# A fused two-block transformer kernel: the recurrent mixer's inputs are loaded ahead of the conditioning chunks, and the chunks' products move later

## The reference, cut to what matters

```python
# block 1
h = rms_norm(x, g_mix); proj = h @ w_in            # 24 column blocks; some for the attention, some for RWKV
r, d_w, k, v, d_a, d_g = split(token_shift_mix(proj_rwkv, mu))     # p + (prev - p) * mu
decay = exp(-exp(-softplus(-(w0 + tanh(d_w) @ w_decay_up)) - 0.5))
a = sigmoid(a0 + d_a @ w_aicl_up);  g = sigmoid(d_g) @ w_gate_lora_up
kk = k * k_k;  kk = kk / max(sqrt(sum(kk * kk)), 1e-12)            # per head of 64: the "key root"
k = k * (1 + (a - 1) * k_a);  b = kk * a
# per head: state = state * decay - (state kk) b^T + v k^T ;  y = state r ; group norm, bonus, times g
x = x + concat(y_dsa, y_rwkv) @ w_out;  x = x + moe(rms_norm(x))
# block 2 uses
mod = silu(c) @ w_ada + b_ada                      # w_ada: 2048 x 12288, six parts of 2048 columns
```

## Time and profile before

| | |
|---|---|
| median of 3 runs | 3314.17 us (3312.25 to 3314.31) |
| the profiled execution | 3311.56 us, its span 3309.3 us |
| mean granted TensorE clock | 0.971 of full |
| PE busy | 94% of the span |
| end of the input projection's matmuls | about 446 us |
| first transposes of `rwkv` (line 962) | 539.7 us |
| pairwise products of `rwkv` (line 977) | 555.0 us |

### The profile page before, as it was taken

The page is one execution under the profiler, slowest core; times in us unless marked ns, Lnnn a source line. Parts: engine busy times, 40 slices in busy tenths (PEclk is TensorE's granted clock), DMA queues, the critical chain, the costliest instruction groups (busy, mean ns, idle before and its releaser), DMA issues. The chain is left out here.

```text
span 3309.3 us, 43832 instructions
## 1 busy us (share of the span) xinstructions
PE 3100.6 (94%) x17864; PEld 2459.1 (74%) x17864; DVE 2067.7 (62%) x2331; ACT 1508.7 (46%) x1819; POOL 20.1 (1%) x10
## 2 busy tenths in 40 slices
PE   8999957979899999999999998999998999999997
PEld 7888844947677676666688876787776788888886
DVE  4557536354677868685548857765575655555555
ACT  4335422223465656564444455455444444444443
POOL 0000001100000000000000000000000000000000
PEclk9999978989899999999999999999999999999999
DMA  7989876076787879696276653475665655555552
GB/s 270 331 274 329 274 263 249 4 296 233 259 315 267 313 256 341 229 320 212 93 248 209 208 194 126 163 241 172 240 230 191 209 185 190 186 182 190 185 183 76
DMA packets 358321, 739.09 MB, mean 223 GB/s; under 512 B 19977, under 2 KB 118422, under 8 KB 344583
## 3 DMA queue, kind: packets, MB, share of 16 engines
q1 hardware_dynamic: 342916, 711.64, 62.5%
q10 hardware_dynamic: 15236, 25.06, 2.1%
HBM read 710.00 MB, written 26.65 MB: 223 GB/s over the span
## 5 line engine op out<-in xcount | busy, mean ns | idle before, releaser
L286 DVE TENSOR_TENSOR moe_w_lo<-ring,moe_w_hi 128x1024 fp32r<-128x1024 f32 x384 | 464.0, 1222 | 174.5 <-ACT moe_w_hi L276 165.4
L286 DVE TENSOR_TENSOR mx_w_lo<-ring,mx_w_hi 128x1024 fp32r<-128x1024 f32 (+1 forms) x288 | 347.5, 1210 | 307.9 <-ACT mx_w_hi L276 303.7
L276 ACT CAST moe_w_hi<-ring 128x1024 fp32r<-128x1024 f32 x384 | 402.3, 1049 | 285.0 <-PE psum L302 281.3
L276 ACT CAST mx_w_hi<-ring 128x1024 fp32r<-128x1024 f32 (+1 forms) x288 | 297.5, 1037 | 448.0 <-PE psum L302 432.0
L286 DVE TENSOR_TENSOR mlp_w_lo<-ring,mlp_w_hi 128x1024 fp32r<-128x1024 f32 x256 | 313.5, 1225 | 293.1 <-ACT mlp_w_hi L276 292.0
L276 ACT CAST mlp_w_hi<-ring 128x1024 fp32r<-128x1024 f32 x256 | 268.4, 1049 | 418.2 <-PE psum L302 418.2
L302 PE MATMUL psum<-mx_w_hi,mx_a_hi 128*128 128x496 f32 (+1 forms) x1024 | 405.6, 396 | 6.4 <-DVE mx_w_lo L286 4.6
L302 PE MATMUL psum<-mx_w_lo,mx_a_hi 128*128 128x496 f32 (+1 forms) x1024 | 397.6, 388 | 0.0
L302 PE MATMUL psum<-mx_w_hi,mx_a_lo 128*128 128x496 f32 (+1 forms) x1024 | 397.6, 388 | 0.0
L286 DVE TENSOR_TENSOR in_w_lo<-ring,in_w_hi 128x628 fp32r<-128x628 f32 x192 | 155.3, 813 | 185.8 <-ACT in_w_hi L276 184.6
L302 PE MATMUL psum<-in_w_hi,in_a_hi 128*128 128x314 f32 x768 | 244.1, 318 | 1.4 <-DVE in_w_lo L286 1.2
(11 more groups left out here) (596 smaller groups left out, 5594.6 us busy)
## 6 DMA issues: line engine op xcount, KB each, us to landing
ring<-in_w_ada SPq DMA_DIRECT2D x72, 1024.0 KB, 7.6
ring<-in_w_e_gate SPq DMA_DIRECT2D x64, 1024.0 KB, 5.4
ring<-in_w_e_up SPq DMA_DIRECT2D x64, 1024.0 KB, 6.3
ring<-in_w_e_down SPq DMA_DIRECT2D x64, 1024.0 KB, 5.2
ring<-in_w_up SPq DMA_DIRECT2D x64, 1024.0 KB, 5.2
ring<-in_w_down SPq DMA_DIRECT2D x64, 1024.0 KB, 5.1
ring<-in_w_in SPq DMA_DIRECT2D x64, 992.0 KB, 5.1
ring<-in_w_in SPq DMA_DIRECT2D x96, 628.0 KB, 5.5
```

The costliest lines, as they stand in the source:

```text
L276: self.nc.scalar.copy(self.w[0][:, self._half(j, half), :, 0:cols], self.view[:, slot, ks, 0:cols]).then_inc(self.hi_done, 1)
L286: self.nc.vector.tensor_tensor(self.w[1][:, q, :, 0:cols], self.view[:, j % self.slots, ks, 0:cols], self.w[0][:, q, :, 0:cols].bitcast(F3 ...
```

## The change

SP no longer asks for chunks 48 to 55 at the end of `first_stream`. It asks for them in `rwkv`, after all inputs of that stage. On ACT the root moves ahead of the two gate copies, and `ada.leave` goes behind the twelve transposed copies. On PE the four chunks at the start and the two behind each gate product are gone. The eight behind the decay sums stay (they are now chunks 48 to 55). Four follow transpose group 14 and four follow group 15. The wait for the copy out of bank 7 moves from ahead of the pairwise products to ahead of group f = 3 of them.

```diff
 # first_stream, SP, at its end
                 sp.wait_ge(da.ov_left, len(da.pairs))
-                ring.first(sp, next_weights)
                 sp.wait_ge(zeroed, 16)
                 in_dram(sp, blocks)
 # program
-        ada.begin()
         rwkv(chip, actT, ada, src["wout"])
 # rwkv, SP, behind the last input
                 sp.dma_start(masks[:], d["consts"][:, RW0:HG0]).then_inc(masks_in, 16)
+                chip.ring.first(sp, ada.source)
+                ada.begin()
                 ada.load(sp, 72)
 # rwkv, ACT
+                root(nc, stat[:], norm[:], asked, rooted)
                 for t in range(T):
                     sc.wait_ge(made, 5 + t)
                     nc.scalar.copy(gate[:, t]..., bank[:, 4:6]...).then_inc(gate_left, 1)
-                root(nc, stat[:], norm[:], asked, rooted)
...
-                ada.leave(sc)
                 for f in range(12):
                     ...
+                ada.leave(sc)
 # rwkv, PE
-                ada.use(pe, 4)
                 pe.wait_ge(small, 2)
...
                         mm = nc.tensor.matmul(bank[:, 4 + b], low[0:LG - P, 3, tt], gup2[:, n], ...)
                     mm.then_inc(made, 1)
-                    ada.use(pe, 2)
...
                     if f == 15:
+                        ada.use(pe, 4)
                         pe.wait_ge(xT_dve, 1)
...
                     mm.then_inc(xT_turned, 1)
+                ada.use(pe, 4)
                 pe.wait_ge(xT_act, 12)
                 pe.wait_ge(xT_dve, 4)
-                pe.wait_ge(ada.copied, 4)
                 for f in range(8):
                     t, qh, kind = f // 4, f // 2 % 2, f % 2
+                    if f == 3:
+                        pe.wait_ge(ada.copied, 4)
```

More of the change, by code:

```diff
@@ L534, in __init__ @@
         self.bank = lambda part: chip.psum[:, 7]
-    def source_next(self, i, j):
-        return self.source(i, self.SPARE + j)
     def source(self, i, j):
@@ L3248, with first_stream @@
 BLOCKS1 = [9, 10, 11, 12, 13] + list(range(9)) + list(range(14, 24))
-def first_stream(chip, pool, sums, qkT, actT, gain, weights, dst, first_row, ada, next_weights):
+def first_stream(chip, pool, sums, qkT, actT, gain, weights, dst, first_row, ada):
     nc, ring, d, bank = chip.nc, chip.ring, chip.dram, chip.psum
@@ L3420, in program @@
             load_parameters(chip, tiles(0), tiles(1), sums0, qkT[0:1, 0:RW_COLS], src["win"])
-            first_stream(chip, pool, sums0[:], qkT, actT, gain("g_mix"), src["win"], d["proj1"], 1, ada, ada.source_next)
-        ada.begin()
+            first_stream(chip, pool, sums0[:], qkT, actT, gain("g_mix"), src["win"], d["proj1"], 1, ada)
         rwkv(chip, actT, ada, src["wout"])
```

## The result

Measured beside each other, the changed kernel takes 3295.4 us (median of 5 runs, 3289.0 to 3297.1) and the kernel before 3312.3 (3309.9 to 3314.3): a ratio of 0.9949, interval 0.9938 to 0.9960, that is 16.9 us faster, between 13 and 20.5. The forecast was a gain of 24. A second comparison gave 0.9955 (0.9941 to 0.9969). The profiled execution took 3297.05 us, its span is 3294.8. One execution of one later experiment, refills in the loop, took 12970 us instead of some 3300; it is in no ratio, and its cause is unknown.

A forecast was written before the change was run, and what follows sets the result against it. PE was busy 94%, so gains lay in its stalls: DMA queue, LoRA inputs, key root. 22.4 us at the pairwise products plus 1.6 for clock made 24: 3311.56 to 3287.6, carried to the median 3290; range 3282 to 3303.

The forecast's parts named there:

- Store: End of the input projection: the last store lands after 2.9 us, first mixer input at 450.3 instead of 457.98.
- narrow inputs: Mixer inputs on an empty queue: DVE's first shift at 456.7, 17.5 us earlier than 474.19.
- LoRA products, sigmoids: PE's LoRA products begin at 469.7, not 487.2; 18.3 us to the fourth sigmoid unchanged, ending at 488.0, not 505.5.
- root: Key root on ACT ahead of the gate copies: DVE resumes at 489.6 instead of 521.96, 32.4 us earlier.
- Gate products and decay sums: PE behind the sigmoids: gate products 6.4 + 1.1 + 5.2 = 12.7 us, to 500.7; decay sums 3.7, to 504.4.
- the rule on a standing PE: Skill's rule that PE waiting for a DMA falls to half clock; the forecast expected little loss from it here.
- second rival: Half clock from the gates on, through decay sums and first eight chunks: gain 9.6 us, 3305; chance 0.11.
- Eight chunks: Behind the decay sums on PE: no wait for landing, 8.7 us, to 513.1, where the transposes start.
- groups, other eight: Transpose groups 0 to 14 take 9.6 us; then four chunks, group 15 and four chunks, to 532.6.
- the clock term: Transposes and first pairwise products follow a busy PE instead of an idle one: 1.6 us gained, between 0 and 3.
- Nothing lost: Behind the pairwise products: refills may delay v, but v has 34 us of slack, so no time is lost.
- four signs of being wrong: Narrow inputs after 462, PE waiting on chunks, clock at 0.50 from 488 to 513, second half of the mixer stretching.

The follow-up runs named there:

- refills in the loop: Changed kernel, with SP asking for chunks 64 to 71 only at the sixth product of the inversion loop: ratio 0.9975 to the kernel before.
- root alone: Kernel before with one edit, ACT doing the key root ahead of the two gate copies: ratio 0.9971, 9.6 us faster.
- root put back: Changed kernel with the root back behind the gate copies, its loads and chunks still changed: ratio 0.9971 to the kernel before, 9.6 us faster.
- filled kernel: Changed kernel with eight unneeded products added on PE behind each of the two gate products: ratio 0.9929 to the kernel before, 23.5 us faster.
- 16 MB moved: Kernel before, with SP storing sixteen 1 MB slots to scratch DRAM once the inversion loop has begun: ratio 1.0053, 17.5 us slower.
- early fill: Changed kernel with chunks 2, 2, 2, 6, 4, late lam exponential, and unneeded products before the first transposes and LoRA products: ratio 0.9926 to before.

## Why the prediction was right, and where its sizes were off

*Store, narrow inputs, LoRA products, sigmoids, root.* Each came within 0.8 us of the forecast. The store landed early, everything moved with the queue, and DVE's wait for the root went as said. The run of the root alone and the one with the root put back price these two halves at 9.6 us each, by themselves.

*Gate products and decay sums.* The mis-sized term. Forecast 5.2 and 3.7 us; measured 8.1 and 7.0. I had bounded the gate product by 8.4 but left the sums at full clock, and had judged the rule on a standing PE by the chunks at 458, in front of a long wait, instead of by the two chunks between the gate products. In the filled kernel the two terms are 4.4 and 3.7. The Trainium skill ("TensorE: Matmul & The Clock Gate", "HAM oscillation — how this bites in real kernels") describes how a PE that waits for a DMA between groups of products falls back to half clock, each time. The traces agree in direction only. With the gap open the sums take 6.99 us in four kernels, with it filled 3.73 in three; but this gap is 1.1 us, a wait for ACT, and in two of the four the clock was at half before it. My second rival was thus half true, for the gates and sums, and false for the chunks (8.80 us, as before).

*Eight chunks, groups, other eight.* The chunks began 5.3 us late, and so did their refills. PE then waited 0.9 and 1.4 us for the last two chunks, which the forecast excluded only with its own earlier start. The groups 0 to 14 took 7.3 us instead of 9.6, the clock term that I had put at 1.6, and the four chunks and group 15 took 4.2 instead of 5.5. Net at the products: 18.9 instead of 22.4. That the sum came so near is partly luck: these gains made up for part of the 5.3 us.

*Behind the products.* "Nothing lost" failed. I had looked only at v, whose transfer indeed had slack. What I had not priced is PE's supply of instructions: with the eight refills, loads now fill the DMA engines from 512 to 560 us, beside the pairwise products and the first steps of the loop, where before they ended at 549, beside the chunks and the transposes. The loop took 52.9 us instead of 50.8; 1.3 of the 2.1 us are the one step with the issue gap of 1.1. The two experiments with moved and added traffic show the cause of that gap. Another 1.3 us are lost between the loop's last copy and the first output copy and 1.1 behind the mixer; the trace names only small gaps there (two of 0.2 put down to issue), and I leave these open. 1.1 us is also within what two executions differ by.

*The signs.* The forecast named four signs of being wrong. One stayed away: the narrow inputs landed in time. The other three came: PE waited for two chunks, the clock stood at half from 489.5 to about 513, and the second half of the mixer grew by 3.4 us. The time lies in the stated range all the same, since the parts that carry the gain, store, queue and root, were right.

## What to carry to other kernels

When a change takes filler work out of a place where an engine waits, price the next stretch at both of TensorE's clocks, and judge a filler by what stands right behind it. Work in another queue can be put beside a wait only once its own data is there: the same loads, reordered without moving their products, cost 7 us. Where no useful work fits a gap, products that nothing needs can pay: they gave 3 us at the products here. And place bulk transfers beside long instructions or beside a stretch that another engine paces: a stretch of short matmuls loses time to full DMA engines though it reads nothing from them.

## What the runs showed of the hardware

Full DMA engines hold up PE's instructions. In the loop PE works through 36 matmuls and as many weight loads a microsecond; with 16 MB moved beside it, 52 and 39 matmuls were left of 144 in two of the windows above. The page's DMA section for that run lists the instruction queue beside the data queue, on the same 16 engines:

```profile
q1 hardware_dynamic: 345220, 728.42, 63.6%
...
q8 instruction: 122, 2.00, 0.2%
```

The records of that queue and of PE say more. Behind the first pairwise product, every wait of 0.4 us or more that is put down to issue stands at one of a row of counts, numbering PE's matmul records from the first: 3388, 3516, 3644, 3772 and so on, 126 to 128 apart, with as many weight loads between. That holds in every kernel here, also in the two with 32 and 96 records added ahead of it, where other instructions stand at these counts. In the changed kernel, in the one with the refills in the loop and in the one with 16 MB moved, each of the twelve waits that cost 1 us or more ends 2.2 to 2.6 us after a 16 KB packet of the instruction queue has started; the packet itself takes about 1 us. So PE goes on when its next block of instructions has come. The row of that queue in the window of 590 to 610 us, in the kernel before and then with 16 MB moved:

```profile
q8 instruction: 6, 0.10, 1.9%
...
q8 instruction: 3, 0.05, 0.9%
```

Before, the blocks came every 3.6 us on average in the loop and PE had no such wait; beside the stores the next ones started 6.6 to 7.0 us apart. The packets take no longer there, so it is their start that comes late; where in between the time goes, the trace doesn't show.

The Trainium skill ("Runtime: NRT & Kernel Launch", "Instruction fetch mechanics") says that instructions are fetched in blocks over a DMA queue of their own and that this is hidden by the pace of issue. The first is in line with the row above; the second holds in the loop of the kernel before, which has no such wait, and does not hold beside the stores, where the loop grew from 50.8 to 67.9 us.

The clock can fall on a PE that is busy. A window of the kernel before (columns as in the earlier trace rows), behind its decay sums:

```profile
526.00:528.00 2.00, 2.00 (x12) 0.39 (x8) 1.97 (x2) 0.00 (x0) 0.00 (x0) 0.50 0.72 217
```

In the kernel before, in the one with the gaps filled and in the one with the early fill the decay sums ran at full clock (3.73 us), with products of two columns each and PE busy all the time, and the chunks right behind them ran partly at half clock (8.7 us for eight chunks in the kernel before; 2.84 us for two in the early fill kernel, 1.92 at full clock). And a gap alone doesn't settle it: 1.1 us between the gate products was followed by half clock in four kernels, in two of which it had fallen before the gap, while in the early fill kernel gaps of 1.2 us at 481 and 488 left it at full. What exactly makes it fall stays open.
